# One value load per expert, idle-time products on TensorE, and a later key/value weight load in a two-layer diffusion trunk

## The reference

```python
for l in range(DEPTH):                                   # DEPTH = 2
    mod_l = (silu_c @ ada_w[l] + ada_b[l]) ...           # 6 modulation rows of 1024, latent and context
    h_l = modulate(rmsnorm(x_l, norm_mix_g[l]), sh1_l, sc1_l)
    ...                                                  # layer 0: RG-LRU | Conformer, layer 1: attention
    x_l = x_l + g1_l * y_l
    ...
    f = grouped_moe(tokens, router_w, router_bias, exp_w_gate[l], exp_w_up[l], exp_w_down[l])
    x_l = x_l + g2_l * f[...]
```

## Time and profile before

| | |
|---|---|
| median of 3 runs | 949.49 us (948.44 to 949.92) |
| the profiled execution: its time, its span | 949.44 us, 947.6 us |
| mean granted clock of TensorE | 0.932 |
| busy: PE, DVE, ACT, POOL | 811.6, 450.0, 268.9, 199.3 us |
| moved by DMA | 309.23 MB, mean 326 GB/s |
| layer 0 experts, first product to last | 283.4 to 528.5 us |
| layer 1 experts, first product to last | 718.1 to 937.8 us |

### The profile page before, as it was taken

How to read it: one execution, slowest core, us unless ns; L and a number is a source line. 1 busy time by engine, 2 the same in 40 slices (tenths; PEclk the granted TensorE clock), 3 DMA queues, 4 the chain that set the end, 5 groups by cost and what they waited for, 6 DMA issues and landing times.

```text
span 947.6 us, 31620 instructions
## 1 busy us (share of the span) xinstructions
PE 811.6 (86%) x13344; PEld 541.6 (57%) x13345; DVE 450.0 (47%) x1104; ACT 268.9 (28%) x474; POOL 199.3 (21%) x364
## 2 busy tenths in 40 slices
PE   3799999999929999999789589999986897586896
PEld 2444444444428777877568445468444675465674
DVE  2379999953564444443234353765262221121232
ACT  2313535431412222332223131255032121111222
POOL 2200000010044444443324510000005221111220
PEclk9999999999959999999899789999988898788998
DMA  9995399376384999999999999974658999999991
GB/s 345 350 386 194 114 376 332 122 285 261 142 332 127 402 407 406 407 411 410 405 410 405 358 382 324 405 291 155 266 180 318 404 400 415 426 420 425 420 391 45
DMA packets 70705, 309.23 MB, mean 326 GB/s; under 512 B 9752, under 2 KB 10192, under 8 KB 54256
## 3 DMA queue, kind: packets, MB, share of 16 engines
q1 hardware_dynamic: 54608, 275.78, 73.9%
q0 software_dynamic: 15040, 30.22, 9.2%
q10 hardware_dynamic: 992, 2.26, 0.6%
HBM read 297.38 MB, written 14.20 MB: 329 GB/s over the span
## 4 chain that ended last, share of the span: by engine, by line
DMA 42%; PE 32%; DVE 19%; issue 3%; SPq 2%; ACT 2%; DVEq 0%; POOLq 0%; POOL 0%
DMA weight_ring<-in_exp_w_down 9%; DVE arena L1083 9%; DMA weight_ring<-in_exp_w_gate 9%; DMA weight_ring<-in_exp_w_up 8%; PE ps L622 7%; PE ps L792 7%; DMA arena<-in_exp_w_up 5%; DMA hT<-in_exp_w_down 3%; DMA arena<-in_exp_w_gate 3%; PE ps L802 3%; PE ps L850 2%; DMA weight_ring<-in_ev_w_in 2%; PE ps L588 2%; SPq L372 2%; PE ps L927 2%
## 5 line engine op out<-in xcount | busy, mean ns | idle before, releaser
L792 PE MATMUL ps<-weight_ring,arena 128*32 128x128 f32 x5760 | 181.9, 284 | 26.0 <-issue 12.2
L792 PEld LDWEIGHTS ps<-weight_ring,arena 128*32 128x32 f32 x5760 | 170.4, 115 | 41.7 <-issue 24.3
L1770 ACT ACTIVATE arena<-ps 128x64 f32<-128x64 f32 x128 | 28.7, 224 | 352.4 <-PE ps L792 352.4
L1375 DVE TENSOR_TENSOR arena<-arena,ps 128x64 f32<-128x64 f32 x128 | 28.2, 221 | 206.8 <-ACT arena L1770 203.6
L588 PE MATMUL ps<-hT,weight_ring 128*128 128x512 f32 x256 | 114.7, 604 | 2.7 <-DMA weight_ring<-in_ev_w_in 2.4
L802 PE MATMUL ps<-weight_ring,arena 128*32 128x256 f32 x1440 | 96.0, 393 | 5.1 <-DMA weight_ring<-in_exp_w_down 2.1
L792 PE MATMUL ps<-arena 128*32 128x128 f32 x2432 | 78.9, 289 | 21.4 <-DMA arena<-in_exp_w_up 19.9
L1083 DVE SCALAR_TENSOR_TENSOR arena<-arena,par 128x512 f32<-128x512 f32 x132 | 94.8, 749 | 4.0 <-DVE arena L1114 0.8
L792 PEld LDWEIGHTS ps<-arena 128*32 128x32 f32 x2432 | 74.6, 117 | 27.2 <-issue 25.3
L588 PEld LDWEIGHTS ps<-hT,weight_ring 128*128 128x128 f32 x256 | 48.2, 192 | 67.2 <-issue 62.8
L1770 ACT ACT_TABLE_LOAD x64 | 82.1, 1283 | 7.7 <-DVEq L1340 2.6
(11 more groups left out here) (320 smaller groups left out, 883.6 us busy)
## 6 DMA issues: line engine op xcount, KB each, us to landing
weight_ring<-in_ada_w SPq DMA_DIRECT2D x24, 2048.0 KB
weight_ring<-in_exp_w_up SPq DMA_DIRECT2D x22, 2048.0 KB, 17.5
weight_ring<-in_exp_w_down SPq DMA_DIRECT2D x22, 2048.0 KB
weight_ring<-in_exp_w_gate SPq DMA_DIRECT2D x22, 2048.0 KB
arena<-in_exp_w_up SPq DMA_DIRECT2D x10, 2048.0 KB
arena<-in_exp_w_gate SPq DMA_DIRECT2D x10, 2048.0 KB
hT<-in_exp_w_down SPq DMA_DIRECT2D x10, 2048.0 KB
weight_ring<-in_ev_w_in SPq DMA_DIRECT2D x4, 2048.0 KB
```

The source lines that it names most:

```text
L792: last = mm(ps[32 * qd:32 * qd + 32, 1 + hh, 0:P].rearrange("p (m n) -> p m n", m=2), xgT[:, MT * k:MT * k + MT], w2[:, k, :, at:at + 64], ...
L1375: v.tensor_tensor(act_in[:, half], act_sl[:, half], ps[:, 1 + hh, 64:P], ALU.mult).then_inc(s_ac[l], 1)
L1770: s.activation(act_sl[:, 64 * hh:64 * hh + 64], ps[:, 1 + hh, 0:64], ACT.Silu).then_inc(s_sl[l], 1)
```

## The change

Four edits:

1. `tile_ends` becomes `tile_end(e)`, one load. `router` reads only entry 0 (after `s_oh`), and `moe` reads entry e just before the tiles of expert e. Layer 1's loop over trios is gone; both layers have 16 loops written out.
2. `keep_warm(bank, n)` multiplies `ident` with the 256 columns of `rw` n times, a result that nothing reads. In layer 0's router 4 of these stand after the load of entry 0, and 4 after a new wait for `s_rt`, behind L741.
3. Before the transposes of tile 0 in layer 1's input, TensorE waits for `s_yg[0]` (upper rows of tile 0 in), behind its wait for slot 5, and makes 5 of these products.
4. SP asks for the key and value weights (`i == GAP_ADA`) only when all stores to `y_rows` have landed.

```diff
@@ SP, load_mid @@
+                if i == GAP_ADA:
+                    for u in range(AHEAD):
+                        sp.wait_ge(s_yo[u], ((ends[0] + (AHEAD - 1 - u)) >> 2) * 16)
+                    sp.sem_inc(s_par, 1)
                 if i == GAP_ADA + 1:
                     sp.wait_ge(s_yg[CT - 1], 16)
                 sp.dma_start(wide(slot), chunk_src(kind, l, c)).then_inc(landed[slot], 16)
@@ TensorE @@
-            def tile_ends(e0, e1):
-                return [pe.value_load(ctl[0:1, e:e + 1], min_val=1, max_val=MAXTILES) for e in range(e0, e1)]
+            def tile_end(e):
+                return pe.value_load(ctl[0:1, e:e + 1], min_val=1, max_val=MAXTILES)
+            def keep_warm(bank, n):
+                for _ in range(n):
+                    mm(ps[:, bank, 0:256], ident[:, :], rw.rearrange("p k n -> p (k n)"), start=True, stop=True)
@@ router @@
                 pe.wait_ge(s_oh, 2 * l + 1)
-                ends = tile_ends(0, SETS if l else E // 2)
+                end = tile_end(0)
+                if not l:
+                    keep_warm(0, 4)
                 pe.wait_ge(s_oh, 2 * l + 2)
...
                     pe.wait_ge(s_mrow, 2)
-                ends += tile_ends(len(ends), SETS if l else E)
+                if not l:
+                    pe.wait_ge(s_rt, 1)
+                    keep_warm(0, 4)
                 pe.wait_ge(s_wide, l + 1)
@@ moe @@
-                for e in range(len(ends)):
-                    tiles_of(e // SETS, e % SETS, ends[e - 1] if e else 0, ends[e])
-                end = ends[-1]
-                if l:
-                    with pe.Fori(1, TRIOS) as trio:
-                        bounds = [pe.value_load(ctl[0:1, bass.ds(trio * SETS + (b - 1), 1)], min_val=1, max_val=MAXTILES)
-                                  for b in range(SETS + 1)]
-                        for b in range(SETS):
-                            tiles_of(trio, b, bounds[b], bounds[b + 1])
-                    first, end = (pe.value_load(ctl[0:1, e:e + 1], min_val=1, max_val=MAXTILES) for e in (E - 2, E - 1))
-                    tiles_of(TRIOS, 0, first, end)
+                first = 0
+                for e in range(E):
+                    if e:
+                        first, end = end, tile_end(e)
+                    tiles_of(e // SETS, e % SETS, first, end)
@@ layer 1 input @@
             slot = next_chunk()
             for t in range(NT):
+                if not t:
+                    pe.wait_ge(s_yg[0], 16)
+                    keep_warm(3, 5)
                 tile_transposes(t)
```

More of the change, by code:

```diff
@@ L757, in router @@
                     residual_rows(4)
-                return ends
+                return end
             def combine_tile():
@@ L766, in combine_tile, with moe @@
                 last.then_inc(s_cb, 1)
-            def moe(l, ends):
+            def moe(l, end):
                 pe.wait_ge(s_red, state["ada"])
```

## The result

The changed kernel is slower: 956.02 us (median of 4 runs, 955.26 to 956.87) against 949.47 us for the kernel before (948.44 to 949.92), a ratio of 1.0076 with a 95% interval of 1.0062 to 1.0090. The prediction was 949.3 us with a range up to 952.3: wrong by 6.7 us, and on the wrong side. The profiled execution of the changed kernel has a span of 955.2 us (before: 947.6) at a mean granted clock of 0.944.

What follows compares the result with a forecast made beforehand. Weight loads by DMA bound both layers' expert stretches, so only TensorE's places around them could pay. The terms -1.15 - 0.35 + 1.26 - 0.8 + 0.3 + 0.6 = -0.14 on 949.44 gave 949.3 us, range 946.0 to 952.3.

Steps and rivals of the forecast that it cites:

- Loads out of the router: Layer 0's router: with the value loads gone, L741 starts right behind VectorE, gaining 1.15 us (1.0 to 1.3).
- Products in the router: Layer 0's router: eight idle-time products cost nothing and may raise TensorE's clock, gaining 0.35 us on average (-0.6 to +3.4).
- neither case of the forecast: Layer 0's router: clock rises before L752, gaining 3.4 us at best, or no earlier than now, taking back 0.6.
- Expert changes in layer 0: Layer 0's experts: a load at each change costs TensorE 0.42 us at three changes, 1.26 lost (0 to 1.8).
- Layer 1's tail: Layer 1's expert change 14 to 15: one load instead of two and a trio's end, gaining 0.8 us (0.2 to 0.85).
- the nine loop bodies: Layer 1's experts: nine more loop bodies in the code must be fetched, losing 0.3 us (0 to 1.0).
- The passage: Between the layers: the store lands earlier, but late weights and five products lose 0.6 us (2.4 won to 5 lost).
- Rival 3: Passage between the layers: weights land late, about 548, delaying products and transposes 4 us, 953.3 us; chance 0.22 with other overruns.

Runs made afterwards that it cites:

- the fourth set: Four kernels against the kernel before: whole change 1.0098; with weights asked early 0.9987; TensorE waiting for weights after tile 0's transposes 1.0035; late ask plus that wait alone 1.0033.

## Why the prediction was wrong

Term by term, in the order of its sum.

- **Loads out of the router, -1.15**: right. L752 starts 0.11 us behind VectorE's one-hot matrix (271.76 + 1.22 = 272.98 in the kernel after) and 1.36 earlier than before; L765 1.39 earlier (1.15 and 1.2 forecast).
- **Products in the router, -0.35**: neither case of the forecast came. The clock rose ahead of the tiles and fell again within the first. The gain at the second tile is 2.31 - 1.36, about 1 us, in this profile. In three profiles of the whole change the eight records of the second group take 3.75, 1.97 and 1.97 us and the first tile 5.37, 6.34 and 6.43: most of what is won ahead of the tiles is lost in the first. Counted from the mask sums, the second tile starts 23.9 us later in the kernel before, 23.0 with edit 1 alone, and 21.8, 22.1 and 23.0 in these three, so the products won 1.3 us, 0.9 or nothing there. Where the clock rose already in the first group (in the windows at 271 and 273 us), the second group was done sooner and TensorE stood 1.66 us behind it, and the clock fell again at 278 and 280. Only one kernel's profile kept full clock through the first tile. The Trainium skill (TensorE: Matmul & The Clock Gate, The HAM clock gate) says that the moment of the rise differs from run to run. Three profiles of one kernel agree: it came in the windows at 278, 271 and 273 us. No run shows that the products pay: edit 1 alone gives 0.9999, with the products 0.9980 and 1.0001.
- **Expert changes in layer 0, +1.26**: the place is right, about 0.4 us each at the two changes of the tail, as forecast. That taking them away gains anything is not shown; 0.1% can't be told.
- **Layer 1's tail, -0.8, and the nine loop bodies, +0.3**: together -0.5 forecast, -1.5 from the last gate ask in the profile. The direction held, the size was low. Ahead of that ask, two times 0.7 us were lost, one before and one within layer 1's weight stretch; whether the loop bodies have a part in it was not tried.
- **The passage, +0.6**: this step failed. Measured +9.2 in the profile. Everything else sums to -1.6 where -0.74 was forecast.

What the passage step got right: the store lands sooner (4.25 us against 6.8), the third gather starts at 533.99 instead of 537.91, the gathers take over 7 us, and the transposes wait for the five products. Tile 0's product ran at full clock and gave nothing, as forecast: it took 7.13 us instead of 8.83, and tile 1's product began 12.05 us behind its start instead of 11.90. The step failed in one number: "The weights, 2 MB among 3 to 4 MB of gathers, land like the chunk asked for at 544.43, whose queue was free again 9.39 us later". They landed 18.9 us after the ask, at 552.26 instead of 543.5 to 545. Three things were wrong in it.

1. The chunk of the earlier trace rows was no model. Beside it stood only what was left of the gathers; and 9.39 us was the time until SP could issue again, which is no landing: in the kernel after, the three chunks asked for at 544.46 have 10.13 us in that column, and a median of 16.1 us from issue to landing. The prediction's own bytes would have told: 2.1 MB of weights and 4.2 MB of gathers at the 374 to 395 GB/s of the windows before are 16 to 17 us, from 533.3 about 550, and this is an estimate; with its 3 MB of gathers it would still be 547. Pieces of 2 KB beside rows of 4 KB put the weights at the end of that. With 1 MB the landing is halved, with 16 KB pieces it comes over 6 us sooner at the gathers' cost.
2. The hole was not seen. The prediction had chunk 3 still landing until 534 and the engines "free" for one us; but in the kernel before it came at 534.15 with the weights in flight beside it. Without them it was in at 530.9, and from 528 to 532 the engines were busy a third of their time or less.
3. The wait for the weights was priced only as a delay of the products. Rival 3 had this right: from 543.5 "each us of delay costing one". With the landing at 552.26 in place of 544 its rule gives 949.3 + 8.3 = 957.6, against 956.0 measured. The mechanism was in the list of rivals, and its landing, "about 548", was sized by an order of queues (gathers first) instead of by bytes and shares. The argument against it, that gathers are not served first, fits the runs (their median rose from 5.7 to 9.5 us) and is beside the point: sharing is enough.

By the fourth set, some 6 us of the loss are the order of the waits. Some 4 are weights that land too late in any order, and the hole explains them by an estimate only.

## What to carry to other kernels

Before a load is made to wait so that others get through, count the bytes that must be moved from then on until it is needed, divide by the rate of the windows, and ask what the engines do in between: a load held back opens a hole of up to its own bytes if nothing else is queued, and those bytes may come back on the path. Take a landing from a row of a landing under the same company, not from the time until the queue was free. And put filler work ahead of a wait for the latest transfer, never behind it: the same five products cost nothing that showed when the weights were in, and stood 3.75 us on the path behind a late landing, with 1.1 of transposes behind them.

## What the runs showed of the hardware

- 2 MB in pieces of 2 KB, asked for as the third of eight gathers of 128 rows of 4 KB was about to start, landed 17.4 to 20.3 us after the ask in seven profiles, 1 MB in 10.3. In pieces of 16 KB they landed within 12.4 us, and the gathers' median went from 9.5 to 11.6.
- With nothing behind them in the queues, the engines were nearly idle (104 and 10 GB/s) in the last 3 us before TensorE went on. Whether the completion or a few late pieces take that time is open.
- TensorE's clock rose in the router at 278 us and fell to half (1.2 GHz) at 282, just as the first tile had begun: TensorE had been busy 0.60 and 0.41 of the windows at 280 and 281. In the one profile that kept full clock through the first tile it had been busy 1.00, 0.68 and 1.00 at 279 to 281.
- A lead can fade: 5.2 us ahead at the second tile were 3.9 at tile 1's product, 2.1 at layer 1's weight stretch and 0.6 at the end, and nothing in the median. Two profiles of one kernel (edits 1 and 2) had spans of 949.4 and 944.6 us, so a single profile's lead of some us is no result.
